# PEER layers with 400 dense token columns in place of 416, and their queue orders rewritten

## The reference

```python
N_KEYS = 128; N_EXPERTS = N_KEYS * N_KEYS; PEER_HEADS = 8; PEER_TOPK = 16
def one_block(xb):                       # 128 tokens
    q = (xb @ w_q).reshape(PEER_BLOCK, PEER_HEADS, 2, PEER_HALF)
    s1 = einsum('thd,kd->thk', q[:, :, 0], sub_k1)
    s2 = einsum('thd,kd->thk', q[:, :, 1], sub_k2)
    v1, i1 = lax.top_k(s1, PEER_TOPK)
    v2, i2 = lax.top_k(s2, PEER_TOPK)
    # cand = all 16 x 16 sums v1 + v2; the expert is i1 * N_KEYS + i2
    top_s, top_pos = lax.top_k(cand, PEER_TOPK)
    gate = jax.nn.softmax(top_s, axis=-1)
    act = jax.nn.gelu(einsum('thkd,td->thk', expert_u[eidx], xb))
    return einsum('thk,thkd->td', gate * act, expert_v[eidx])
```

## Time and profile before

| | |
|---|---|
| runs of the kernel, median (lowest to highest) | 3673.15 us (3670.6 to 3678.32) |
| span of the profiled execution | 3715.8 us |
| PE busy | 3517.8 us, 95% of the span, 21277 matmuls |
| PE weight loads busy | 3348.0 us, 90% |
| DVE busy | 2481.2 us, 67% |
| POOL busy | 1842.5 us, 50% |
| ACT busy | 1361.9 us, 37% |
| DMA | 812.36 MB, mean 219 GB/s |

### The profile page before, as it was taken

The page is one execution under the profiler, slowest core; times in us unless marked ns, Lnnn a source line. Parts: engine busy times, 40 slices in busy tenths (PEclk is TensorE's granted clock), DMA queues, the critical chain, the costliest instruction groups (busy, mean ns, idle before and its releaser), DMA issues.

```text
span 3715.8 us, 61775 instructions
## 1 busy us (share of the span) xinstructions
PE 3517.8 (95%) x21277; PEld 3348.0 (90%) x21277; DVE 2481.2 (67%) x5400; ACT 1361.9 (37%) x1938; POOL 1842.5 (50%) x1172
## 2 busy tenths in 40 slices
PE   7999999999999999999888689999999999999998
PEld 7999999999999999999773359999999999999998
DVE  3342597777775777775678543679697876777774
ACT  3322343534444333333221353344435353333332
POOL 3434456555655555552541234456565655555551
PEclk9999999999999999999998699999999999999999
DMA  3222367877788999994346322467777879999982
GB/s 131 80 69 91 103 188 247 277 247 262 262 281 274 298 310 313 324 320 154 99 116 179 105 74 91 136 193 249 268 240 277 274 282 277 297 326 311 329 295 97
DMA packets 392484, 812.36 MB, mean 219 GB/s; under 512 B 52104, under 2 KB 249672, under 8 KB 384888
## 3 DMA queue, kind: packets, MB, share of 16 engines
q1 hardware_dynamic: 171600, 458.35, 37.0%
q0 software_dynamic: 64608, 230.73, 18.1%
q10 hardware_dynamic: 156048, 120.37, 11.0%
HBM read 695.39 MB, written 112.74 MB: 217 GB/s over the span
## 4 chain that ended last, share of the span: by engine, by line
PE 66%; DVE 16%; DMA 7%; issue 4%; ACT 2%; POOL 2%; SPq 2%; another core or an unknown queue 0%; ACTq 0%; DVEq 0%; POOLq 0%
PE acc L638 42%; PE acc L625 15%; DMA rows<-u_in,expertP 4%; PE misc L774 3%; DVE rows L1838 3%; DMA raw<-slabs_in 2%; POOL w_lo L2274 1%; DVE misc L1773 1%; DVE route L1777 1%; DVE hot_gate L1876 1%; PE misc L814 1%; ACT w_hi L1104 1%; DVE work L1716 1%; DVE keyi L1724 1%; PE misc L843 1%
## 5 line engine op out<-in xcount | busy, mean ns | idle before, releaser
L2274 POOL TENSOR_TENSOR w_lo<-raw,w_hi 128x1024 fp32r<-128x1024 f32 x365 | 892.6, 2446 | 1079.8 <-ACT w_hi L1104 1078.6
L638 PE MATMUL acc<-h_hi,w_hi 128*128 128x416 f32 x3072 | 1097.7, 357 | 0.2 <-POOL h_lo L2316 0.2
L638 PE MATMUL acc<-h_lo,w_hi 128*128 128x416 f32 x3072 | 1085.9, 353 | 0.0
L638 PE MATMUL acc<-h_hi,w_lo 128*128 128x416 f32 x3072 | 1081.2, 352 | 0.0
L1104 ACT ACTIVATE w_hi<-raw 128x1024 fp32r<-128x1024 f32 x617 | 653.3, 1060 | 1090.0 <-DMA raw<-slabs_in 1045.4
L638 PEld LDWEIGHTS acc<-h_hi,w_hi 128*128 128x128 f32 x3072 | 581.2, 189 | 8.5 <-POOL h_lo L2316 0.6
L638 PEld LDWEIGHTS acc<-h_hi,w_lo 128*128 128x128 f32 x3072 | 581.9, 189 | 7.4
L638 PEld LDWEIGHTS acc<-h_lo,w_hi 128*128 128x128 f32 x3072 | 581.3, 189 | 3.9
L1955 DVE TENSOR_TENSOR w_lo<-raw,w_hi 128x1024 fp32r<-128x1024 f32 x252 | 325.4, 1291 | 206.1 <-ACT w_hi L1104 205.5
L1838 DVE CUSTOM_DVE_ANT_0 rows<-acc,rows 128x1024 f32<-128x1024 f32 (+1 forms) x224 | 273.4, 1221 | 205.9 <-DMA rows<-u_in,expertP 183.7
L638 PE MATMUL acc<-y_hi,w_hi 128*128 128x416 f32 x1024 | 362.1, 354 | 10.3 <-DVE y_lo L1947 4.3
(11 more groups left out here) (349 smaller groups left out, 5549.4 us busy)
## 6 DMA issues: line engine op xcount, KB each, us to landing
raw<-slabs_in SPq DMA_DIRECT2D x617, 512.0 KB
act_d<-gelu SPq DMA_DIRECT2D x256, 208.0 KB
gate_d<-gout SPq DMA_DIRECT2D x52, 1024.0 KB
abuf<-act_d ACTq DMA_DIRECT2D x32, 1664.0 KB
gbuf<-gate_d ACTq DMA_DIRECT2D x30, 1664.0 KB
unit<-ck_in SPq DMA_DIRECT2D x72, 128.0 KB
vquad<-cv_in SPq DMA_DIRECT2D x64, 128.0 KB
unit<-ck_in ACTq DMA_DIRECT2D x56, 128.0 KB
```

What stands on the lines that cost most here:

```text
L638: last = pe.matmul(acc[:, 0, par, 0:ND], w[:, c, :], m(c), start=c == 0 and w is w_hi[r] and m is m_hi, stop=c == KC - 1 and w is w_lo[r])
L2274: pool.tensor_tensor(w_lo[r][:], raw[r][:], w_hi[r][:].bitcast(F32), ALU.subtract).then_inc(lo_done, 1)
```

## The change

- ND goes from 416 to 400, so 112 prompt tokens go by gathered rows: 128 dots and 128 values in a layer instead of 112, and 50 half chunks of gates instead of 52.
- The first block has no gate steps. The windows are 20, 20, 16 and 16 slabs, the steps 16, 16 and 16, and the last two halves stand behind slabs 120 and 121.
- The scores of the next block are computed two pairs of heads' banks at a time inside the steps of the block before (behind steps 5 and 9; for block 1 behind slabs 19 and 21 of the first windows).
- `count_row` is gone: the one-hots read `iota` from SBUF, and PSUM bank 3 is free for scores.
- Each row fetch is issued one slab after the dot that frees its buffer, not two slabs before its use, but none of the prompt rows before slab 27.
- SP's route detour stands after slab 24 instead of slab 20.
- `act_d` and `gate_d` have other layouts: a group's load reads longer runs, the store of a gate chunk writes runs of 512 B. A group's two loads are now eight parts, spread over its slabs 0 to 6. The gate steps' last chunks are loaded at slab 124 instead of 121.
- Values run 12 in 11 slabs, and `group_y` follows by `GROUP_END`.
- DVE weighs and splits group 0 before it waits for the gelu of the dots.

```diff
-ND = 416
+ND = 400
-        act_d = [nc.dram_tensor(f"act_d{l}", [NK, P, ND], F32).ap() for l in range(2)]
-        gate_d = [nc.dram_tensor(f"gate_d{l}", [NG, P, NK, TG], F32).ap() for l in range(2)]
+        act_d = [nc.dram_tensor(f"act_d{l}", [NK // 4, P, 4, ND], F32).ap() for l in range(2)]
+        gate_d = [nc.dram_tensor(f"gate_d{l}", [NK // GRP, P, NG, GRP, TG], F32).ap() for l in range(2)]
...
-        ROUTE_SLABS = [20, 16, 16, 16]
-        SLAB0 = [sum(ROUTE_SLABS[:b]) + STEP0[b] for b in range(NDB)]
+        ROUTE_SLABS = [20, 20, 16, 16]
+        HALF_STEPS = 16
+        SLAB0 = [0, 20, 56, 88]
...
-        WINDOW_DOTS = 12
-        STEP_DOTS = [[1] * 4, [1] * 4 + [0, 0] + [2, 1, 2, 1, 2, 2, 1, 2, 1, 2]]
...
-        FETCH_AT = [n - 2 for n in at_slab]
+        WINDOW_DOTS = [16, 10, 10, 10]
+        STEP_DOTS = [1, 2] * (HALF_STEPS // 2)
...
+        FETCH_AT = [5] * RB + [n + 1 for n in at_slab[:-RB]]
+        FETCH_AT = [n if i < TOPK else max(n, 27) for i, n in enumerate(FETCH_AT)]
...
+                def scores(b, pair):
...
                     if b:
-                        pe.wait_ge(gate_taken, 2 * (H0 + STEP0[b]) + 2)
-                        pe.wait_ge(slotT_done, B)
+                        pe.wait_ge(score_taken, 4 * B + 2 * pair)
...
+                    for r in range(HALF_STEPS):
+                        s_slab(0, done[0])
...
+                        gates(H0 + HALF_STEPS * (b - 1) + r, r % 2)
+                        if r in (5, 9) and b + 1 < NDB:
+                            pe.wait_ge(slotT_done, l * NDB + b + 1)
+                            scores(b + 1, r // 9)
...
+                        if j + 2 < J:
+                            for part in range(2) if c == 0 else range(c + 1, min(c + 2, 8)):
+                                load_part(j + 2, par, part)
...
-            count_row = misc[:, 3, 0:P]
...
-                dve.tensor_tensor(hot1[par][:], count_row.unsqueeze(1).to_broadcast([P, HG, P]),
+                dve.tensor_tensor(hot1[par][:], iota[:].unsqueeze(1).to_broadcast([P, HG, P]),
                                   idxT[:, 0, t0:t0 + HG].unsqueeze(2).to_broadcast([P, HG, P]), ALU.is_equal)
                 for t in range(HG):
-                    last = dve.tensor_scalar(hot_gate[par][:, t, :], count_row, idxT[:, 1, t0 + t:t0 + t + 1],
+                    last = dve.tensor_scalar(hot_gate[par][:, t, :], iota[:], idxT[:, 1, t0 + t:t0 + t + 1],
                                              gateT[:, t0 + t:t0 + t + 1], ALU.is_equal, ALU.mult)
```

More of the change, by code:

```diff
@@ L465, in build @@
         assert len(FETCH_AT) == OPS
+        GROUP_END = [next(n for n in range(NK) if values_by(n) >= (g + 1) * TOPK) for g in range(NGR)]
+        assert GROUP_END[-1] + 5 <= NK - 6
         N_CONST = 10
@@ L827, in peer @@
                     last.then_inc(routeT_done, 1)
[L828 to L833, removed]
+                scores(0, 0)
+                for j in range(2, 4):
+                    for k in range(4):
+                        ht = 4 * j + k
+                        last = pe.matmul(misc[:, j, k * P:(k + 1) * P], qT[:, ht, 0:P], subk[:, 2 * l + ht % 2, :],
+                                         start=True, stop=True)
+                    last.then_inc(score_done, 1)
+                pe.wait_ge(s_sc_taken, l + 1)
+                s_only(2)
+                group_h(0)
+                s_only(17)
+                scores(1, 0)
+                s_only(2)
+                scores(1, 1)
+                s_only(2)
+                group_h(1)
+                s_only(1)
+                turn_route(0)
+                s_only(SLAB0[1] + ROUTE_SLABS[1] - done[0])
+                for b in range(1, NDB):
+                    turn_route(b)
+                    if b == 1:
+                        pe.wait_ge(score_taken, 4 * (l * NDB + 2))
+                    for r in range(HALF_STEPS):
+                        s_slab(0, done[0])
+                        done[0] += 1
+                        if (b, r) in starts:
+                            group_h(starts[b, r])
+                        gates(H0 + HALF_STEPS * (b - 1) + r, r % 2)
+                        if r in (5, 9) and b + 1 < NDB:
+                            pe.wait_ge(slotT_done, l * NDB + b + 1)
+                            scores(b + 1, r // 9)
+                    if b + 1 < NDB:
+                        s_only(ROUTE_SLABS[b + 1])
+                for r, n in enumerate(LAST_STEPS):
+                    s_slab(0, n)
+                    gates(H0 + 3 * HALF_STEPS + r, r % 2)
+                done[0] += len(LAST_STEPS)
                 s_only(NK - done[0])
@@ L1370, in peer @@
                                 square(2, i)
[L1371 to L1372 removed]
+                        if n - 1 in GROUP_END:
+                            group_out(GROUP_END.index(n - 1))
             def attention():
@@ L1956, in weight_low @@
                         lo_done, 1)
+                for c in range(GRP):
+                    weigh(0, c)
+                for c in range(GRP):
+                    low_part(0, c)
                 dve.wait_ge(dot_act_done, 2 * (l + 1))
```

272 lines of the change are left out of this document (153 added, 119 removed).

## The result

The changed kernel takes 3932.72 us (3927.67 to 3935.17, four runs) against 3675.74 us for the one before on the same chip: ratio 1.0705 (95% interval 1.0686 to 1.0724), where 0.971 was forecast. The experiments ran on four chips, each beside the kernel before, which has medians of 3709 to 3716 us there, so they are given as ratios. Run again on one of the four, the changed kernel stands at 1.0732 (a_same).

What follows compares the result with a forecast made beforehand. PE was taken to set the pace. Work of -89.0 us and waits of -17.7 gave -106.7 on the profiled span, 3609.1; times 0.9885, 3568 us, with a range of 3530 to 3635.

Steps and rivals of the forecast that it cites:

- Columns: Dense slabs on PE: 16 fewer columns save 0.171 us a slab, giving 4.369 us, 87.6 us in all.
- Fetches issued as a buffer comes free should end most of the 92.9 us for rows: DVE's waits for gathered rows mostly end; on PE that was 7.3 us of late one-hots at the most.
- 6 us a layer for the steps and 7.5 for block starts: PE's waits in phase s, per layer: 6 us in gate steps, 2.5 at each of three block starts.
- The port: Gate steps: SBUF one-hots held by `w_lo`; rival with half unhidden, 1.2 us a step, 54 us less 12, 3609; chance 0.20.
- the rival for the other sign: Slower than before: port in gate steps wholly unhidden, a step takes 7.88 us, 168 us less 12, 3722; chance 0.05.
- The clock: Phase s: 2 us a layer of lower clock added behind PE's gap at the detour.
- The factor from span to time: Whole kernel: profiled span of 3609.1 us multiplied by 0.9885, median of runs over span, giving 3568 us.
- Waits that go: DVE's 31.4 us for scores and PE's 12.7 us for the route go, and most of DVE's 92.9 for rows.
- The detour: Phase s, SP's route loads: PE stands 9 us a layer plus 2 of lower clock; five fetches ahead of `w_lo` add 4.
- The turn to phase y: End of phase s: PE waits 4.7 us a layer, last gates loaded three slabs later, ten dots ahead of `weigh`.
- Phase y: Work falls 20.1 us to 574.0, waits left at 5 us a layer.
- the bound that the rival had: DMA bounds phase y: at 318 GB/s a slab takes 4.74 us, 86 us in all, 3653; chance 0.08.

Runs made afterwards that it cites:

- a_fetch_s: Changed kernel with row fetches in phase s issued two slabs before their dot at the latest: ratio 1.0272.
- b_fetch: Kernel before, with phase s row fetches issued not before the slab behind the dot that frees their buffer, as in the changed kernel: ratio 1.0395.
- c_early: c_start with `group_h` put back behind the slab of its step: ratio 1.0105.
- c_start: c_psum with dots 0, 1, 2, 2, 1, ... in a block's steps, so none ahead of the first one-hots: ratio 0.989, the fastest.
- a_group_h: Changed kernel with `group_h` of a gate step ahead of the step's dense slab, not behind it: ratio 1.0679.
- b_iota: Kernel before, with both one-hots reading `iota` from SBUF and not `count_row` from PSUM: ratio 1.0202.
- a_all3: Changed kernel with the edits of a_fetch_s, a_fetch_y and a_group_h together: ratio 1.0125.
- c_psum: a_all3 with one-hots reading `count_row` from PSUM again, scores in banks 0 and 1 and PE waiting for ACT's copies: ratio 0.9914.
- a_psum: Changed kernel with only c_psum's edit, one-hots reading `count_row` from PSUM and scores in banks 0 and 1 with waits: ratio 1.0748.
- a_fetch_y: Changed kernel with rows of v in phase y fetched two slabs before use, not as soon as their buffer is free: ratio 1.0653.

## Why the prediction was wrong, step by step

- **Columns: right.** 4.37 us a slab in the windows, forecast 4.369.
- **"Fetches issued as a buffer comes free should end most of the 92.9 us for rows": wrong, the step that failed.** I read the rule as early, which it is in the windows (4 to 6 slabs). In the steps, at 1.5 dots a slab and four buffers, the dot four earlier is 2 or 3 slabs back, and one slab behind it leaves one slab for 21 of the 72 dots in the steps, where there were two. I had counted the fetches' place in POOL's queue at slab 27 only, not in the steps. On the table of numbers alone it could be seen. I put 6 us a layer for the steps and 7.5 for block starts; the steps of layer 0 took 465.5 us against 294.2 + 6 x 0.96 + 2 x 3.84 = 307.6 of work, so 158 in place of 13.5. Shown by a_fetch_s (-0.046) and b_fetch (+0.040).
- **`group_h` inside the step: not seen.** I counted it as 1 us of work. As the last link ahead of DVE's dots it is worth 0.0215 once the rows are early and the port is out of the way (c_early against c_start), 0.003 to 0.005 before (a_group_h).
- **The port: seen, and judged too lightly.** The rival had 54 us for it; b_iota (75 us) and a_all3 to c_psum (0.0211, 78 us) measured more. I gave the port 0.25 in all because the one-hots would fit between two `w_lo`; they met one in 72 of 104 half steps (b_iota). In the changed kernel it cost nothing that a_psum shows. So the rival for the other sign, which I built on the port, had the sign and not the cause.
- **The clock: mis-sized.** I allowed 2 us a layer behind one gap; phase s of layer 0 lost 47 at a granted clock of 0.92.
- **The factor from span to time: unfounded.** I multiplied by 0.9885 because the profile of before lay 42 us over the median. The profiled execution of the changed kernel took 3927.7 us for a span of 3925.9, with an attention stage 45 us shorter than in the profile of before. So the 42 us probably are that stage (not shown, as the profiled execution of before has no time of its own), and had to be subtracted. That both ways take off about 41 us here is luck.
- **Waits that go: right for the route on PE** (12.7 to 1.6 us). DVE's wait for scores went, too.
- **The detour: right in size.** Slabs 27 to 29 took 11.44 + 6.94 + 5.34 us, 10.6 over 3 x 4.37; forecast 9 + 2. With slabs 30 to 32 it is 14.9 over; forecast 15 with the five fetches. To hide it failed each time.
- **The turn to phase y: mis-sized.** From slab 120 on 17.6 us over the work in place of 4.7. The order is visible in the changed kernel: ACT waited 13.6 us for `weigh`, which stood behind ten dots, and DVE waited 10.4 us in one go for the row of one of these, fetched one slab ahead. With earlier fetches it is 12.6 over the work (a_fetch_s), still not 4.7. What would mend the rest was not found.
- **Phase y: wrong.** Forecast 579 us, measured 595.9 and 592.4. How much of it the late fetches of v make is not settled (a_fetch_y), nor what holds the rest, with PE waiting for `y_lo` and `h_lo` at group ends. DMA at 0.84 and 294 GB/s of mean was not the bound that the rival had: a window's bound would show in most slabs, and most took 4.37 to 4.39.

With late fetches, `group_h` and port taken out, c_start stands at 0.989, so part of the columns' gain is there. It is 0.018, some 66 us, short of the forecast. By its profile 27 us of that lie in the gate steps, 15 at the turns to phase y, 12 in phase y and 12 in the windows; the detour costs it what was forecast. The new layouts, the spread loads, the order of the scores and the windows were never undone one by one, so what each is worth is not shown.

## What to carry to other kernels

A rule that ties a prefetch to "when its buffer comes free" is early only where the consumers are sparse: write out the distance from issue to use for each item, for the densest stretch above all. With in-order queues on four engines, each wait is passed on to everything behind it, so look for the loop (what the late item's producer itself waits for), and put nothing that only the partner engine can release between two halves of a hand-over. One cause hides the next: two edits that were worth 0.005 and nothing alone were worth 0.02 each once the other causes were gone, so a single edit without effect clears nobody. Nor is it enough to take out the largest: with only the rows early the kernel would stand near 1.02 (estimate: a_fetch_s less the gain of a_fetch_y), with `group_h` moved too at 1.0125 (a_all3), with the one-hots in PSUM instead at 1.0105 (c_early, with c_start's table), and with both at 0.989 (c_start).

## What the runs showed of the hardware

- A DVE instruction with its operands in SBUF is held by a GpSimd tensor_tensor beside it (eight hot_gates 4.24 for 2.13 us in b_iota); with its tensor operand in PSUM it isn't (832 hot_gates, none over 0.408 us, though 418 of them ran beside a `w_lo`).
- The clock makes a wait dearer. In the changed kernel 50 of the 100 groups of 16 gate matmuls came behind waits of 3.0 to 6.2 us of PE and took 2.5 to 3.8 us; the 50 others came behind 1.1 us at most and took 1.95 to 2.05.
- A fetch of gathered rows issued by POOL in phase s of the changed kernel landed 3.8 to 10.1 us after its issue, 6.0 in the median.
- The changed kernel's attention stage lasted 547.5 us in its first profile, at a granted clock of 0.95, and 591.1 in a_same, at 0.90. The profile of before has 592.5, at 0.90. Whether the chip makes the difference is not shown.
